# The opening of a 256-token, two-block transformer kernel in another order: weights and activations in pieces, warm-up matmuls, squares shared with GpSimd

## The reference

```
h   = concat(meta, x)                                  # 272 tokens x 1024
n   = h * rsqrt(mean(h*h, axis=-1) + eps) * ffn1_norm
gu  = n @ ffn1_w_in                                    # 1024 x 5632
h   = h + 0.5 * (silu(gate) * up) @ ffn1_w_out
```

## Time and profile before

| | us |
|---|---|
| device time, median of 3 runs | 1059.12 |
| the three runs | 1058.96, 1059.12, 1060.35 |
| span of the profiled execution, first to last instruction | 1056.1 |
| median less that span | 3.0 |
| TensorE matmuls busy in the span | 1019.6 (97%) |

### The profile page before, as it was taken

One profiled execution on the slowest core, in us unless ns is written; L12 is line 12 of the kernel. 1 busy time (PEld: TensorE's weight loads), 2 busy tenths in 40 slices (PEclk: granted clock), 3 DMA queues, 4 the chain that ended last, 5 costly groups with the idle time before them and its releaser, 6 DMA issues.

```text
span 1056.1 us, 21171 instructions
## 1 busy us (share of the span) xinstructions
PE 1019.6 (97%) x8000; PEld 982.2 (93%) x8000; DVE 688.7 (65%) x1252; ACT 508.4 (48%) x832; POOL 31.1 (3%) x49
## 2 busy tenths in 40 slices
PE   4999999999999999999999999999999999999996
PEld 4999999989987789999999999887899999999996
DVE  4666664555676548776666548979666378885543
ACT  5544453363455545655444448341664365543431
POOL 4200000010100000000000000000000000000000
PEclk8999999999999999999999999999999999999998
DMA  6445465437732224655556456313454255556551
GB/s 218 160 178 172 167 230 178 150 118 237 239 120 92 90 80 141 200 193 185 180 200 232 166 184 214 120 61 120 165 174 141 100 180 183 191 184 199 169 189 42
DMA packets 46544, 172.71 MB, mean 164 GB/s; under 512 B 5498, under 2 KB 7682, under 8 KB 45968
## 3 DMA queue, kind: packets, MB, share of 16 engines
q1 hardware_dynamic: 44160, 162.58, 45.1%
q0 software_dynamic: 1360, 8.57, 2.5%
q10 hardware_dynamic: 960, 0.67, 0.2%
HBM read 170.72 MB, written 3.77 MB: 165 GB/s over the span
## 4 chain that ended last, share of the span: by engine, by line
PE 87%; DVE 7%; ACT 3%; issue 2%; DMA 1%; DVEq 0%; ACTq 0%
PE bank L384 26%; PE bank L386 25%; PE bank L385 25%; DVE cy L1291 3%; DVE wlo L365 1%; ACT whi L354 1%; PE bank L396 1%; PE bank L1089 1%; PE bank L779 1%; PE bank L781 1%; DMA res<-in_res 1%; PE bank L1474 1%; PE bank L1451 1%; PE bank L753 1%; PE bank L752 1%
## 5 line engine op out<-in xcount | busy, mean ns | idle before, releaser
L384 PE MATMUL bank<-xhi,whi 128*128 128x256 f32 (+1 forms) x1464 | 423.3, 289 | 10.9 <-DVE wlo L365 10.2
L386 PE MATMUL bank<-xhi,wlo 128*128 128x256 f32 (+1 forms) x1464 | 416.4, 284 | 0.0
L385 PE MATMUL bank<-xlo,whi 128*128 128x256 f32 (+1 forms) x1464 | 415.4, 284 | 0.0
L365 DVE TENSOR_TENSOR wlo<-raw,whi 128x1024 fp32r<-128x1024 f32 (+1 forms) x287 | 362.9, 1266 | 24.1 <-ACT whi L354 23.8
L354 ACT ACTIVATE whi<-raw 128x1024 fp32r<-128x1024 f32 (+1 forms) x287 | 311.5, 1086 | 129.6 <-PE bank L386 110.8
L384 PEld LDWEIGHTS bank<-xhi,whi 128*128 128x128 f32 x1464 | 277.4, 189 | 18.4 <-issue 17.5
L385 PEld LDWEIGHTS bank<-xlo,whi 128*128 128x128 f32 x1464 | 277.7, 190 | 0.2
L386 PEld LDWEIGHTS bank<-xhi,wlo 128*128 128x128 f32 x1464 | 277.4, 189 | 0.0
L384 PE MATMUL bank<-hid_hi,whi 128*128 128x256 f32 (+1 forms) x608 | 172.9, 284 | 0.0
L385 PE MATMUL bank<-hid_lo,whi 128*128 128x256 f32 (+1 forms) x608 | 172.6, 284 | 0.0
L386 PE MATMUL bank<-hid_hi,wlo 128*128 128x256 f32 (+1 forms) x608 | 171.8, 283 | 0.0
(11 more groups left out here) (258 smaller groups left out, 1163.5 us busy)
## 6 DMA issues: line engine op xcount, KB each, us to landing
raw<-in_w_f1in SPq DMA_DIRECT2D x44, 512.0 KB, 3.5
raw<-in_w_f2in SPq DMA_DIRECT2D x44, 512.0 KB, 3.5
raw<-in_w_mix SPq DMA_DIRECT2D x35, 512.0 KB, 3.5
raw<-in_w_up SPq DMA_DIRECT2D x32, 512.0 KB, 3.6
raw<-in_w_down SPq DMA_DIRECT2D x32, 512.0 KB, 4.1
raw<-in_w_f1out SPq DMA_DIRECT2D x16, 704.0 KB, 4.1
raw<-in_w_f2out SPq DMA_DIRECT2D x16, 704.0 KB, 4.2
raw<-in_w_mixb SPq DMA_DIRECT2D x20, 512.0 KB, 3.5
```

What stands on the lines that cost most here:

```text
L365: nc.vector.tensor_tensor(wlo[:, s, 0:tiles * P], raw[:, s, 0:tiles * P], whi[:, s, 0:tiles * P], ALU.subtract).then_inc(w_lo, 1)
L384: nc.tensor.matmul(out, whi[:, s, w], rhs_hi(t), start=start and t == 0, stop=False)
L385: nc.tensor.matmul(out, whi[:, s, w], rhs_lo(t), start=False, stop=False)
L386: mm = nc.tensor.matmul(out, wlo[:, s, w], rhs_hi(t), start=False, stop=stop and t == tiles - 1)
```

## The change

Strip one is loaded in two halves of 4 tiles and split half by half; `res` comes in four pieces of two tiles, three on ScalarE's queue and one on SP's, in full rows of 288 columns (the host pads them). `ident` is issued ahead of `vecs`. ScalarE runs one Sqrt before its first copy. Thirteen 128x128 matmuls of ones go ahead of strip one on TensorE, into a bank that nothing reads before it is written anew. GpSimd squares tiles 0 to 3 and adds them up in `sg`, in seven operations ahead of its own loads; ScalarE squares tiles 4 to 7 only, behind strip two's `whi`, and VectorE makes three additions of these and one of GpSimd's sum, behind strip two's and strip three's `wlo`. On TensorE `pe_stat` moves from behind strip one to behind strip two, and `pe_norm` from behind strip two to behind strip three. The counts that later waits use are changed to fit (`readied`, `added`), in `dve_square` too, which isn't shown. Context lines are cut.

```diff
@@ -54,6 +54,7 @@
 LEAD = 3
+WARM = 13
 WIDE = 11
@@ -256,7 +257,9 @@
         norm_sd, norm_inv, norm_bc, norm_r = (sem(s) for s in ("norm_sd", "norm_inv", "norm_bc", "norm_r"))
-        res_low, res_high = sem("res_low"), sem("res_high")
+        res_in = [sem(f"res_in{i}") for i in range(4)]
+        head_in, head_hi, head_lo = sem("head_in"), sem("head_hi"), sem("head_lo")
+        pool_sq = sem("pool_sq")
         gain_in, vec_in, ident_in = sem("gain_in"), sem("vec_in"), sem("ident_in")
@@ -411,9 +414,17 @@
 
+        def readied(n):
+
+            return KT * n - HALF if n else 0
+
+        def added(n):
+
+            return (KT - 1) * n - 3 if n else 0
+
         def pe_stat(pe, n, full):
 
-            pe.wait_ge(sq_added, (KT - 1) * (n + 1))
+            pe.wait_ge(sq_added, added(n + 1))
             if n:
@@ -428,7 +439,7 @@
             static = isinstance(m, int)
-            before = (KT - 1) * n + max(m - 2, 0) if static else m + ((KT - 1) * n - 2)
+            before = added(n) + max(m - 2, 0) if static else m + (added(n) - 2)
             if static and m == 0:
@@ -443,7 +454,8 @@
 
-            dst = sqsum if isinstance(m, int) and m == 0 else sq[:, par, :]
+            opens = isinstance(m, int) and m == (0 if n else HALF)
+            dst = sqsum if opens else sq[:, par, :]
             nc.scalar.activation(flat_or_two(dst, full), res_tile(m, full), ACT.Square).then_inc(sq_ready, 1)
@@ -491,6 +503,14 @@
 
+        def wait_start(pe):
+
+            def before(t):
+                if t == HALF:
+                    pe.wait_ge(w_lo, 1)
+                pe.wait_ge(x_lo, t + 1)
+            return before
+
 
@@ -498,14 +518,16 @@
                 for j in range(4):
-                    pe.wait_ge(w_lo, splits(c0 + 4 * i + j, c0 + j))
+                    head = edge and i == 0 and j == 0
+                    opening = head and n == N_F1
+                    if not opening:
+                        pe.wait_ge(w_lo, splits(c0 + 4 * i + j, c0 + j))
                     out = start_group(pe, g0, 4, i, j)
-                    head = edge and i == 0 and j == 0
-                    strip(out[:, 0:width], (c0 + j) % RING, KT, hi, lo,
-                          before=wait_x(pe, n) if head else None).then_inc(pe_done, 1)
-                    if head:
+                    before = (wait_start(pe) if opening else wait_x(pe, n)) if head else None
+                    strip(out[:, 0:width], (c0 + j) % RING, KT, hi, lo, before=before).then_inc(pe_done, 1)
+                    if edge and i == 0 and j == (1 if n == N_F1 else 0):
                         pe_stat(pe, n, width == T)
-                    if edge and i == 0 and j == 1:
+                    if edge and i == 0 and j == (2 if n == N_F1 else 1):
                         pe_norm(pe, n, width == T)
@@ -1623,8 +1645,9 @@
         def _(sp):
-            sp.dma_start(res[:, 0:HALF, 0:T], io["res"][:, 0:HALF, :]).then_inc(res_low, 16)
-            sp.dma_start(raw[:, 0, 0:KT * P], io["w_f1in"][0]).then_inc(w_in[0], 16)
+            sp.dma_start(raw[:, 0, 0:HALF * P], io["w_f1in"][0][:, 0:HALF * P]).then_inc(head_in, 16)
+            sp.dma_start(raw[:, 0, HALF * P:KT * P], io["w_f1in"][0][:, HALF * P:KT * P]).then_inc(w_in[0], 16)
+            sp.dma_start(res[:, 4:6, :], io["res"][:, 4:6, :]).then_inc(res_in[2], 16)
             for name, n, tiles, *_ in PHASES:
@@ -1663,7 +1686,19 @@
             nc.gpsimd.memset(epsc[:, 1:2], HD * EPS).then_inc(ones_set, 1)
-            pool.wait_ge(res_high, 16)
+            steps = 0
+            for m in range(HALF):
+                pool.wait_ge(res_in[m // 2], 16)
+                if m > 1:
+                    pool.wait_ge(pool_sq, steps)
+                nc.gpsimd.tensor_tensor((hd if m else sg)[:, 0:T], res[:, m, 0:T], res[:, m, 0:T],
+                                        ALU.mult).then_inc(pool_sq, 1)
+                steps += 1
+                if m:
+                    pool.wait_ge(pool_sq, steps)
+                    nc.gpsimd.tensor_tensor(sg[:, 0:T], sg[:, 0:T], hd[:, 0:T], ALU.add).then_inc(pool_sq, 1)
+                    steps += 1
+            pool.wait_ge(res_in[3], 16)
             for dst, name in ((same, "same"), (swap, "swap"), (convw, "convw")):
@@ -1738,22 +1773,29 @@
             act.dma_start(gains[:, :], io["gains"]).then_inc(gain_in, 16)
-            act.dma_start(res[:, HALF:, 0:T], io["res"][:, HALF:, :]).then_inc(res_high, 16)
+            for part in (0, 1, 3):
+                act.dma_start(res[:, 2 * part:2 * part + 2, :],
+                              io["res"][:, 2 * part:2 * part + 2, :]).then_inc(res_in[part], 16)
+            act.dma_start(ident[:, :], io["ident"]).then_inc(ident_in, 16)
             act.dma_start(vecs[:, :], io["vecs"]).then_inc(vec_in, 16)
-            act.dma_start(ident[:, :], io["ident"]).then_inc(ident_in, 16)
+            act.wait_ge(ones_set, 3)
+            nc.scalar.activation(root[:, 3:4], epsc[:, 0:1], ACT.Sqrt)
+            act.wait_ge(head_in, 16)
+            nc.scalar.activation(whi[:, 0, 0:HALF * P], raw[:, 0, 0:HALF * P], ACT.Copy).then_inc(head_hi, 1)
             act.wait_ge(gain_in, 16)
-            act.wait_ge(ones_set, 3)
-            act.wait_ge(res_low, 16)
-            for m in range(KT):
-                if m == HALF:
-                    split_hi(act, 0, 1, 0, 0)
-                    act.wait_ge(res_high, 16)
-                act_x(N_F1, m, True)
-            for m in range(KT):
-                if m % HALF == 0:
-                    split_hi(act, 0, 1, 1 + m // HALF, 0)
-                if m >= 3:
-                    act.wait_ge(sq_added, m - 2)
+            for part in range(4):
+                act.wait_ge(res_in[part], 16)
+                act_x(N_F1, 2 * part, True)
+                act_x(N_F1, 2 * part + 1, True)
+                if part == 0:
+                    act.wait_ge(w_in[0], 16)
+                    nc.scalar.activation(whi[:, 0, HALF * P:KT * P], raw[:, 0, HALF * P:KT * P],
+                                         ACT.Copy).then_inc(w_hi, 1)
+            split_hi(act, 0, 1, 1, 0)
+            for m in range(HALF, KT):
+                if m == HALF + 3:
+                    split_hi(act, 0, 1, 2, 0)
+                    act.wait_ge(sq_added, 1)
                 act_square(N_F1, m, True, m % 2)
@@ -1772,15 +1814,27 @@
         def _(dve):
+            dve.wait_ge(head_hi, 1)
+            nc.vector.tensor_tensor(wlo[:, 0, 0:HALF * P], raw[:, 0, 0:HALF * P], whi[:, 0, 0:HALF * P],
+                                    ALU.subtract).then_inc(head_lo, 1)
             dve.wait_ge(gain_in, 16)
             for m in range(KT):
-                if m == HALF:
-                    split_lo(dve, 0, 1, 0, 0)
                 dve_prep(dve, N_F1, m, True)
-            for m in range(KT):
-                if m % HALF == 0:
-                    split_lo(dve, 0, 1, 1 + m // HALF, 0)
-                dve_square(dve, N_F1, m, True, m % 2)
+                if m == 1:
+                    dve.wait_ge(w_hi, 1)
+                    nc.vector.tensor_tensor(wlo[:, 0, HALF * P:KT * P], raw[:, 0, HALF * P:KT * P],
+                                            whi[:, 0, HALF * P:KT * P], ALU.subtract).then_inc(w_lo, 1)
+            split_lo(dve, 0, 1, 1, 0)
+            for k in range(3):
+                if k == 2:
+                    split_lo(dve, 0, 1, 2, 0)
+                dve.wait_ge(sq_ready, k + 2)
+                if k:
+                    dve.wait_ge(sq_added, k)
+                nc.vector.tensor_tensor(sqsum[:, 0:T], sqsum[:, 0:T], sq[:, (k + 1) % 2, 0:T], ALU.add).then_inc(sq_added, 1)
+            dve.wait_ge(pool_sq, 7)
+            dve.wait_ge(sq_added, 3)
+            nc.vector.tensor_tensor(sqsum[:, 0:T], sqsum[:, 0:T], sg[:, 0:T], ALU.add).then_inc(sq_added, 1)
             dve_ff_in(dve, "f1in", N_F1, T)
@@ -1805,6 +1859,9 @@
             pe.wait_ge(ones_set, 3)
+            for _ in range(WARM):
+                nc.tensor.matmul(ps[7][:, 0:P], ones[:, :], ones[:, :], start=True, stop=True)
+            pe.wait_ge(head_lo, 1)
             pe_ff_in(pe, "f1in", N_F1, T)
@@ -1909,7 +1966,7 @@
     tokens = np.concatenate([x[:P], meta, x[P:]])
-    arrays["res"] = tokens.T.reshape(KT, P, T).transpose(1, 0, 2)
+    arrays["res"] = np.pad(tokens, ((0, W2 - T), (0, 0))).T.reshape(KT, P, W2).transpose(1, 0, 2)
     arrays["mem"] = a["mem_2"][0].T.reshape(KT, P, NX).transpose(1, 0, 2)
```

More of the change, by code:

```diff
@@ L453, in dve_square @@
             width = T if full else NX
-            dve.wait_ge(sq_ready, m + (KT * n + 1))
+            dve.wait_ge(sq_ready, m + (readied(n) + 1))
             if not (isinstance(m, int) and m == 1):
-                dve.wait_ge(sq_added, m + ((KT - 1) * n - 1))
+                dve.wait_ge(sq_added, m + (added(n) - 1))
             nc.vector.tensor_tensor(sqsum[:, 0:width], sqsum[:, 0:width], sq[:, par, 0:width], ALU.add).then_inc(sq_added, 1)
```

## The result

The changed kernel took **1050.79 us** (median of 4 runs, 1049.09 to 1051.52), the kernel before beside it 1059.73 (4 runs); the ratio is 0.9915, 95% interval 0.9898 to 0.9931: by the ratio 9.0 us faster. The forecast was 1055.5 and its range 1051.2 to 1057.4.

The account below looks back on a forecast made before the run. TensorE, busy 97% of the span, was taken as the bound, its opening paying a late start, a norm hole and half clock. Strip five at 27.9 against 31.48 gained 3.6: 1059.1 - 3.6 = 1055.5 us, range 1051.2 to 1057.4.

Parts of the forecast that it names:

- What bounds it: Whole kernel: TensorE is busy 97% of the span, so only a change in its start, stops or slowing moves the end.
- ScalarE's start: Opening: six DMA issues end near 4.0, then a 1.28 us table load and the Sqrt; ScalarE ready at 5.5.
- F: Rival at ScalarE's opening table load: a drain follows, ScalarE starts 1.4 us later than 5.5, total 1056.3; chance 0.04.
- Landings: Opening loads: half strip by 4.7, first activation piece at 4.6, no further wait; up to 1 us if wrong.
- VectorE and GpSimd: Opening: five of GpSimd's seven operations hold VectorE 0.6 us each, 3.0 in all; strip two ready at 15.3.
- B: Rival in the opening: GpSimd does not hold VectorE; VectorE done at 12.3, 7.1 us gained, total 1052.0; chance 0.27.
- TensorE: Opening: strip one 8.1 to 15.6, strip two to 19.3, strip three to 23.0, strip five at 27.9; 3.6 us gained.
- the wait of 1.6 before strip five: After strip four: only one strip covers the fifth strip's split behind the norm, so TensorE waits 1.6 us.
- C: Rival before strip five: the new 1.6 us wait lets the clock fall, losing 1.7 us, total 1057.2; chance 0.10.
- D: Rival in the opening: warm-up forgotten, strips one and two both at 1.2 GHz, fifth strip 28.7, total 1056.3; chance 0.06.
- The steps after it are unchanged: From strip five to the end: nothing changes, so the opening's 3.6 us gain carries to the end.
- The 3.0 that stood between span and median: Whole kernel before: profiled span 1056.1, median 1059.12, 3.0 above it; this difference was carried over into the forecast.

Follow-up runs that it names:

- e4: The changed kernel without GpSimd's squares; ScalarE squares all eight tiles and VectorE makes all seven adds: 1051.14 us, ratio 0.9919 to the kernel before.
- e9: The kernel before with the 13 warm-up matmuls added ahead of strip one, nothing else: 1058.23 us, ratio 0.9996.
- e10: The kernel before with four small GpSimd operations ahead of the copies of the bias rows, which delays them: 1058.51 us, ratio 0.9996.
- e1: The kernel before, unchanged, measured again: 1060.01 us, ratio 1.0008.

## Why the prediction was wrong in size

**What bounds it** held: TensorE's share is as large as before, and the end followed the opening.

**ScalarE's start** was forecast at 5.5; its Sqrt ran at 5.70 and the first copy at 5.80, since the issues of its queue ended at 4.4 and not 4.0. From the table load's start to the next activation 1.30 passed, and F falls. The 2.66 of the Trainium skill (ScalarE: Activation LUTs, What ACT_TABLE_LOAD costs) is not seen in this trace either.

**Landings** were a little worse: xhi waited 0.27, 0.85 and 0.30 for res, 1.4 in all, where no further wait had been taken (up to 1 if wrong), and GpSimd, put at 4.6, began at 6.68. The last xlo ended at 14.17 all the same, against 14.1; that this fits so well is luck, by two errors that cancel (next).

**VectorE and GpSimd** hold each other up: 0.91 became 1.40 for two tiles of xlo and 0.68 became 1.25 for a half strip. The trace agrees with the Trainium skill (SBUF — State Buffer, Terms), which has the port locked for whole instructions, in that the one slows while the other works; that the lock lasts the whole instruction is not shown by it. All seven operations met VectorE's list, not five, and took less each: the first block, the half strip and the rest of xlo are 2.7 longer than in e4 (1.40 + 1.25 + 4.34 against 0.91 + 0.68 + 1.74 + 0.92), some 0.4 an operation where I had 0.6. Seven at 0.4 gave nearly the 3.0 of five at 0.6. Of these 2.7 only 2.1 arrive at strip two's low part, since in e4 VectorE waited for ScalarE in between. B, with its chance of 0.27, falls.

**TensorE** was forecast step by step: strip one 8.1 to 15.6 (8.08 to 15.47), strip two to 19.3 (18.6: full clock, 3.12, where the middle 3.7 was taken), the square-sum at 18.3 (18.5; the forecast had an add at 0.44, where the earlier trace rows gives 0.55 and so 18.7, which would have changed nothing), strip three to 23.0 (22.4), the wait of 1.6 before strip five (1.51), strip five at 27.9 (27.41). C did not come: the clock stayed up behind that wait in all three profiles. D holds in half: the warm-up was forgotten, but only strip one ran slow.

**The step that failed** is the last: "The steps after it are unchanged", with the 3.6 carried to the end against a single profile. Two terms were mis-sized, the gain of the opening (3.6) and that of all that follows (0). The opening is worth 4.7 by three profiles each, 1.1 more than 3.6: 0.5 is strip two at full clock, 0.3 is that before's first profile started strip five 0.3 earlier than its mean, the rest lies within the scatter of 0.7. And the rest of the kernel is some 2 us shorter with the falls taken out, where nothing was forecast: 0.6 to 0.8 at the end and 0.3 near 405 us, in all ten profiles with the pieces, and 0.5 to 1.9 at the wait for qn, which shrank in e9 and e10 too. By the terms 4.7 + 2 = 6.7. The measured gain is 9.0, 8.6 and 7.0 us by the three ratios, and what lies between I put down to what falls do to medians of 4 to 12 runs; that is not shown, since how often each kernel falls is not settled.

The 3.0 that stood between span and median was two things: about 1.9 lies around the span (1050.74 less 1048.8 for the changed kernel, 1059.63 less 1057.8 in e1), and by it the other 1.1 was that before's profiled execution was faster than the median. Carrying it was right; taking the one profile's 31.48 for the kernel's was the risk.

What stays open: where the 0.3 near 405 us comes from, why a fall follows a given pause in one execution and not in the next, and how much of the pieces' 0.9961 is the change in fetches.

## What to carry to other kernels

Where an engine waits for a by-product (here the square-sum), first move the consumer behind the next piece of work that is ready: in single profiles that edit of two conditions brought 4.1 (to the kernel before) and 4.5 (to the pieces) where the whole change brought 4.7 us in the opening, while GpSimd's squares and the warm-up together brought 2 us without the move and nothing with it. Read the medians beside it: the move alone brought 2.3 there. Before sharing work with GpSimd, set what it takes from VectorE (here 2.1 us at strip two) against what it saves it (here three adds); in this kernel nothing was left. A forecast of a few microseconds in a thousand should take its starting times from more than one profile, and should leave room for the stretch behind the change even if no instruction there is touched.

## What the runs showed that was not expected

The granted clock's row can't be trusted ahead of its first change. Without the warm-up the windows give 1.00 from the start:

```profile
8.00:12.00 4.00, 2.92 (x10) 2.38 (x11) 4.00 (x6) 3.73 (x8) 3.70 (x5) 1.00 0.95 341
16.60:19.00 2.40, 2.40 (x22) 2.40 (x21) 2.18 (x3) 0.00 (x0) 2.21 (x3) 1.00 0.73 224
```

but in the first, at 8.52, a matmul of 272 columns takes 0.43 and the next follows by 0.22, and in strip two 0.29 and 0.13. The durations tell the level there, not the row.

Where instructions are fetched may be a cost of its own: with 26 more matmuls at the start a store 250 us later took 2.3 us longer, and with another order of the opening the last output landed 0.5 us sooner, each time with a fetch beside the slower one.
